# One place more for rounded weight pieces, one fewer for raw weight units, and weight sums taken one unit later

## The chip, the cores and the metric

One core of a Trainium2 chip runs one program. Times are device microseconds of one execution of the whole kernel, the median of several executions. PE is TensorE, DVE is VectorE, ACT is ScalarE, POOL is GpSimd, and SP is the engine that issues most transfers.

## What is computed

Two transformer-like layers over 256 tokens of width 2048, in float32. Everything is a chain of products with weights that are used once, with small attention and recurrence parts between them:

```
proj = rms_norm(x) @ w_in                 # 13 parts: q k v o i f z, two latents, k_r, z_b, g_a, g_b
y_a  = (sigmoid(o) * norm(mlstm(q, k, v)) * silu(z)) @ w_a
y_b  = (attention(latents @ w_uq, latents @ w_ukv) * silu(z_b)) @ w_b
x    = x + (sigmoid(g_a) * y_a + sigmoid(g_b) * y_b) @ w_out
h    = x + concat(fourier_mix, dilated_attention)(rms_norm(x) @ w_in_2) @ w_out_2
h    = h + square(relu(rms_norm(h) @ w_up_2)) @ w_down_2      # d_ff = 8192
out  = rms_norm(h)
```

## The kernel before

**Weights.** All weights are laid out on the host as one stream of 359 units of 1 MB (128 partitions x 2048 floats). SP loads them in order into `raw`, four places. Each unit is cut into pieces of up to 1024 columns, 802 in all. ACT rounds a piece to a float32r high half (L1227, `w_hi`), and DVE subtracts to get the low half (L1827, `w_lo`). PE then makes three products for each block: high x high, high x low, low x high (L659 to L661, L758 to L760). In the feed-forward part ("up" products, `project_up`) it makes one product of twice the width with the high half (L1118) and one with the low half (L1122).

**The ring.** `RING = 4` places hold rounded pieces. The feed-forward part, from piece 490 on, has two places more, `RING_DEEP = 6`, and the last four pieces have places of their own. ACT may round piece n only when PE has used piece n - 4 (n - 6 in the feed-forward part): the wait on `w_used` at L1225. SP loads unit u into the place of unit u - 4 once DVE has made the low halves of that unit's first two pieces (`w_rest`, L496). PE waits for the low half of each piece (`w_rest`).

**Sum units.** In seven pairs of column chunks of the first input product (`pair_in`) and seven pairs of the down product (`pair`), some of the eight steps of a pair replace eight block products by seven, in the manner of Strassen. They need sums of weight blocks, and such a unit has four pieces: a whole and a half piece of raw blocks, and two pieces of sums in `w_sum`. DVE makes the sums with three instructions, `sum_weights` (L1841, L1844, L1845). The kernel before makes the sums of unit u + 1 just behind the low half of the first piece of unit u (L1829). A pair of the down product has sum units at steps 1, 2, 4 and 5 (`SUM_AT`), a pair of the input product at steps 2 and 5 or 3 and 5.

**Order on the engines.** All engines' programs are unrolled and run in order. ACT and DVE go through `pieces(n, slot)`: for each piece that PE uses, they split the piece that stands 4 (6) places ahead, and then do the slot's other work, if any. So the piece that is split beside a given slot, and with it every `sum_weights`, moves when the ring's depth changes; the slot's own place against PE does not.

**Feed-forward part.** Four slabs. Each has eight up chunks (c = 0 to 7) of four pieces, then the down product in two pairs, q = 2n and 2n + 1 (the last slab has one pair and two plain chunks). At the end of an up chunk DVE reads its PSUM banks (L2602, then L2606 squares), and that releases the banks (`proj_read`). The even pair's step 1, its first sum step, writes into banks that chunk 7 used: PE waits there for `proj_read` of all chunks (L1163). At step 5 DVE adds the mixed products (`add_mixed`), and at step 7 ACT drains four banks (`drain_whole`, L1732), before it splits the two pieces of that step. The first two up chunks of the next slab wait for these drains: chunk 0 for the first two (L1181). POOL issues the drained tiles as adding transfers into `nat`.

**Start.** SP's first issues are three units mixed with six parts of the transposed x, a fourth unit, and then the first half of x in natural layout (`nat`), before the loop over the other units.

Of the kernel before, what the change touches and what calls it, by code (L numbers as in the profile page):

```python
# [5 lines left out]
P = 128  # L6
# [11 lines left out]
EPS = 1e-6  # L18
BIG = 1e30
PIECE = 2 * CW  # L20
RING = 4
NORM_FULL = 8
NORM_LORA = 2
NORM_UP = 4
# [3 lines left out]
UNITS = 1 + 4 * (4 + 4 + 8 + 4 + 2 + 8) + 14 + 4 * (4 + 4 + 4) + 4 * 8 + 4 * 4 + 4 * N_SLABS * 8  # L28
# [22 lines left out]
SUM_UNITS = _sum_units()  # L51
# [15 lines left out]
WHERE, FIRST_PIECE = _pieces()  # L67
PIECES = len(WHERE)
DEEP = FIRST_PIECE[UNITS_MLP]
RING_DEEP = RING + 2  # L70


def place_of(piece):

    if piece < DEEP:
        return piece % RING
    if piece >= PIECES - RING:
        return piece % RING + RING_DEEP
    n = (piece - DEEP) % RING_DEEP
    return RING + n if n < 2 else (DEEP + n - 2) % RING  # L80

# [81 lines left out]
def build(nc, stream, x_in, xt_in, consts_in, early_in, params_in, pos_in, dft_in, alibi_in, fg_in, wf_in, z_store, ga_store, gb_store,  # L163
          out):
    f32, f32r, i32 = mybir.dt.float32, mybir.dt.float32r, mybir.dt.int32
# [4 lines left out]
    with ctx:  # L170
# [4 lines left out]
        def place(name, shape, dt, kb):  # L175
            return nc.alloc_sbuf_tensor_at(name, shape, dt, offset=base + int(kb * K))

        raw = place("raw", [P, RING, 2 * PIECE], f32, 0)
        w_hi = place("w_hi", [P, RING, PIECE], f32r, 32)
        w_lo = place("w_lo", [P, RING, PIECE], f32r, 48)  # L180
        a_both = place("a_both", [P, KT, 2, TOK], f32r, 64)
        a_hi, a_lo = a_both[:, :, 0, :], a_both[:, :, 1, :]
        nat = place("nat", [P, TT, D], f32, 96)
# [52 lines left out]
        alibi = place("alibi", [P, H_2, 2 * TOK], f32, 176.25)  # L236
        m_hi = place("m_hi", [P, KT, TOK], f32r, 112)
        m_lo = place("m_lo", [P, KT, TOK], f32r, 128)
        w_hi_end = place("w_hi_end", [P, RING, PIECE], f32r, 64)
        w_lo_end = place("w_lo_end", [P, RING, PIECE], f32r, 80)  # L240
        w_hi_deep = place("w_hi_deep", [P, 2, PIECE], f32r, 144.25)
        w_lo_deep = place("w_lo_deep", [P, 2, PIECE], f32r, 152.25)
        ms_at = [160.25 + 4 * i for i in range(3)] + [190.25]
# [3 lines left out]
        w_sum = place("w_sum", [P, 2, 2 * PIECE], f32, 174.25)  # L247
        fg = place("fg", [P, D], f32, 174.25)
        hi_places = [w_hi[:, i, :] for i in range(RING)] + [w_hi_deep[:, i, :] for i in range(2)]
        hi_places += [w_hi_end[:, i, :] for i in range(RING)]  # L250
        lo_places = [w_lo[:, i, :] for i in range(RING)] + [w_lo_deep[:, i, :] for i in range(2)]
        lo_places += [w_lo_end[:, i, :] for i in range(RING)]

        e_at = 180.25
        early = place("early", [P, N_EARLY], f32, e_at)
# [6 lines left out]
        at = 192.25  # L262
# [4 lines left out]
        at = -(-at * K // 32) * 32 / K  # L267
# [84 lines left out]
        def sem(name):  # L352
            return ctx.enter_context(nc.semaphore(name))
# [3 lines left out]
        early_rounded = sem("early_rounded")  # L357
        early_rest = sem("early_rest")
        early_x = sem("early_x")
        raw_landed = [sem(f"raw_landed{i}") for i in range(RING)]  # L360
        w_rounded = sem("w_rounded")
        w_rest = sem("w_rest")
        w_used = sem("w_used")
# [7 lines left out]
        x_ready = [sem(f"x_ready{i}") for i in range(TT)]  # L371
# [96 lines left out]
        x_v = x_in.rearrange("(t p) d -> p t d", p=P)  # L468
# [4 lines left out]
        @block.sync  # L473
        def _(sp):
            ident_cols = CONSTS["ident"]

            def x_part(i):

                k0, k1 = XT_PARTS[i]
                sp.dma_start(xt[:, k0:k1, :], xt_in[:, k0:k1, :]).then_inc(xt_ready[i], 16)  # L480

            sp.dma_start(raw[:, 0, 0:CW], stream[0][:, 0:CW]).then_inc(first_quarter, 16)
            x_part(0)
            sp.dma_start(raw[:, 0, CW:PIECE], stream[0][:, CW:PIECE]).then_inc(second_quarter, 16)
            x_part(1)
            sp.dma_start(raw[:, 0, PIECE:], stream[0][:, PIECE:]).then_inc(raw_landed[0], 16)
            x_part(2)
            sp.dma_start(raw[:, 1, :], stream[1]).then_inc(raw_landed[1], 16)
            x_part(3)
            sp.dma_start(raw[:, 2, :], stream[2]).then_inc(raw_landed[2], 16)  # L490
            x_part(4)
            x_part(5)
            sp.dma_start(raw[:, 3, :], stream[3]).then_inc(raw_landed[3], 16)
            sp.dma_start(nat[:, 0, :], x_v[:, 0, :]).then_inc(x_ready[0], 16)
            for u in range(RING, UNITS):
                sp.wait_ge(w_rest, FIRST_PIECE[u - RING] + 2)  # L496
                sp.dma_start(raw[:, u % RING, :], stream[u]).then_inc(raw_landed[u % RING], 16)
                if u == RING:
                    sp.dma_start(nat[:, 1, :], x_v[:, 1, :]).then_inc(x_ready[1], 16)
                    sp.dma_start(early[:, :], early_in).then_inc(early_ready, 16)  # L500
                if u == RING + 4:
                    sp.dma_start(cst[:, ident_cols.stop:], consts_in[:, ident_cols.stop:]).then_inc(cst_ready, 16)

            sp.wait_ge(out_ready, 2)
            sp.dma_start(out_v[:, 0, :], nat[:, 0, :]).then_inc(stored, 16)
            for n, c in ((3, 3), (4, 0)):
                cols = slice(c * CW, (c + 1) * CW)
                sp.wait_ge(out_ready, n)
                sp.dma_start(out_v[:, 1, cols], nat[:, 1, cols]).then_inc(stored, 16)
            sp.wait_ge(stored, 16 * 4)  # L510
# [687 lines left out]
        def _(act):  # L1198
            piece, done, chunk, tr, seq = Tally(), Tally(), Tally(), Tally(), Tally()
# [9 lines left out]
            def split(n=1):  # L1209
                for _ in range(n):  # L1210
                    if piece.reg is None and piece.n >= PIECES:
                        return
                    u, at, width, summed = WHERE[piece.n]
                    if piece.n == 1:
                        act.wait_ge(raw_landed[0], 16)
                    elif piece.n == FIRST_PIECE[u]:
                        act.wait_ge(raw_landed[u % RING], (u // RING + 1 if piece.reg is None else piece.cycle(2 * RING)) * 16)
                    src = raw[:, u % RING, at:at + width]
                    if summed:
                        i = SUM_UNITS.index(u)  # L1220
                        act.wait_ge(w_summed, 2 * i + (1 if at == 0 else 2))
                        src = w_sums(i)[:, at:at + width]
                    deep = piece.reg is None and piece.n >= DEEP
                    if not (deep and piece.n >= PIECES - RING):
                        act.wait_ge(w_used, piece.at(RING + 1 - RING_DEEP if deep else 1))  # L1225
                    s = place_of(piece.n) if piece.reg is None else piece.n % RING
                    A(hi_places[s][:, 0:width], src, ACT.Copy).then_inc(w_rounded, 1)  # L1227
                    piece.add()
# [531 lines left out]
            for n in range(N_SLABS):  # L1760
                for c in range(UP_CHUNKS):
# [15 lines left out]
                    b = proj_all[:, 2 * (chunk.n % 2):2 * (chunk.n % 2) + 2, TOK:2 * TOK]  # L1777
# [29 lines left out]
        def _(dve):  # L1807
            piece, done, chunk, tr, seq, his = (Tally() for _ in range(6))
# [8 lines left out]
            def split(n=1):  # L1817
                for _ in range(n):
                    if piece.reg is None and piece.n >= PIECES:
                        return  # L1820
                    u, at, width, summed = WHERE[piece.n]
                    s = place_of(piece.n) if piece.reg is None else piece.n % RING
                    src = raw[:, u % RING, at:at + width]
                    if summed:
                        src = w_sums(SUM_UNITS.index(u))[:, at:at + width]
                    dve.wait_ge(w_rounded, piece.at(1))
                    V.tensor_tensor(lo_places[s][:, 0:width], src, hi_places[s][:, 0:width].bitcast(f32),  # L1827
                                    SUB).then_inc(w_rest, 1)
                    if u + 1 in SUM_UNITS and piece.n == FIRST_PIECE[u]:  # L1829
                        sum_weights(u + 1)  # L1830
                    piece.add()

            def sum_weights(u):

                i = SUM_UNITS.index(u)
                dve.wait_ge(raw_landed[u % RING], (u // RING + 1) * 16)
                b = raw[:, u % RING, :].rearrange("p (b c) -> p b c", b=4)
                s = w_sums(i).rearrange("p (b c) -> p b c", b=4)
                if i > 1:
                    dve.wait_ge(w_rest, FIRST_PIECE[SUM_UNITS[i - 2]] + 4)  # L1840
                V.tensor_tensor(s[:, 0:2, :], b[:, 0:3:2, :], b[:, 3, :].unsqueeze(1).to_broadcast([P, 2, CW]),  # L1841
                                ADD).then_inc(w_summed, 1)
                dve.wait_ge(w_summed, 2 * i + 1)
                chain(V.tensor_tensor(s[:, 2, :], s[:, 0, :], b[:, 2, :], ADD))  # L1844
                V.tensor_tensor(s[:, 3, :], s[:, 2, :], b[:, 1, :], ADD).then_inc(w_summed, 1)  # L1845
# [734 lines left out]
            for n in range(N_SLABS):  # L2580
                for c in range(UP_CHUNKS):
# [18 lines left out]
                    b = proj_all[:, 2 * (chunk.n % 2):2 * (chunk.n % 2) + 2, 0:TOK]  # L2600
# [168 lines left out]
```

## Time and profile before

| | us |
|---|---|
| median of 3 runs | 2095.89 |
| their range | 2095.5 to 2096.8 |
| the profiled execution's own time | 2096.05 |
| its span in the trace | 2094.2 |
| PE busy | 2080.3 |
| DVE busy | 1452.2 |
| ACT busy | 1120.6 |

Read it with care: the matmuls overlap and their ends are modelled, so the busy time of PE does not show a wait shorter than about 0.16 us, the overlap of two neighbours. A steady stream of 512-column products starts one every 0.23 us. The distance between the starts shows what was lost. The part from 1399 us on is the feed-forward part; the pairs of the input product run from about 152 to 449 us.

### The profile page before, as it was taken

Reading aid. Unit: us, or ns where it says so; the run is one execution under the profiler, and the core shown is the slowest. Engines: PE = TensorE matmul, PEld = TensorE weight load, DVE = VectorE, ACT = ScalarE, POOL = GpSimd, SP = SyncE. Lnnn points to the kernel's source line nnn. Section 1 sums busy time; section 2 is a strip of 40 time slices with the busy share of each in tenths; the row PEclk is TensorE's granted clock in tenths of the full one; section 3 lists DMA queues with packets and bytes.
Section 4 is the critical chain, followed back from the end, with each engine's and each line's share of the span. In section 5 each row is a group of like instructions: output and inputs, shape, how many; then the busy total and the mean of one; then the engine's idle time right before and its main releaser. Section 6 shows DMA issues by size and latency. Waiting matters only on the chain.

```text
span 2094.2 us, 25089 instructions
## 1 busy us (share of the span) xinstructions
PE 2080.3 (99%) x10024; PEld 1747.0 (83%) x10024; DVE 1452.2 (69%) x1893; ACT 1120.6 (54%) x1466; POOL 69.5 (3%) x85
## 2 busy tenths in 40 slices
PE   9999999999999999999999999999999999999998
PEld 7888888888888888888888888888888888888886
DVE  6877888875555786556554455566896896797794
ACT  6555555555444675554454454354564565465463
POOL 0000000000000020000000000000010000000000
PEclk9999999999999999999999999999999999999999
DMA  8555455564465544355755542455576477467564
GB/s 334 184 181 209 171 211 210 190 248 177 174 227 201 188 144 161 141 224 198 299 184 185 191 161 101 161 201 182 180 238 232 163 236 237 180 217 256 184 211 133
DMA packets 62196, 413.88 MB, mean 198 GB/s; under 512 B 7040, under 2 KB 7680, under 8 KB 14720
## 3 DMA queue, kind: packets, MB, share of 16 engines
q1 hardware_dynamic: 53856, 382.71, 50.8%
q0 software_dynamic: 7648, 28.84, 4.9%
q8 instruction: 79, 1.29, 0.3%
q10 hardware_dynamic: 576, 0.73, 0.1%
q14 instruction: 37, 0.30, 0.0%
HBM read 394.69 MB, written 8.39 MB: 192 GB/s over the span
## 4 chain that ended last, share of the span: by engine, by line
PE 96%; DVE 1%; ACT 1%; issue 1%; DMA 0%; SPq 0%; POOLq 0%; POOL 0%; DVEq 0%; ACTq 0%
PE proj L659 15%; PE proj L661 15%; PE proj L660 15%; PE proj L1118 11%; PE proj L1122 6%; PE proj L758 4%; PE proj L760 4%; PE proj L759 4%; PE tbank L758 2%; PE tbank L759 2%; PE tbank L760 2%; PE tbank L614 2%; PE bank_a L758 1%; PE bank_a L760 1%; PE bank_a L759 1%; PE bank_b L760 1%
## 5 line engine op out<-in xcount | busy, mean ns | idle before, releaser
L1827 DVE TENSOR_TENSOR w_lo<-raw,w_hi 128x1024 fp32r<-128x1024 f32 (+1 forms) x627 | 740.3, 1195 | 503.3 <-ACT w_hi L1227 496.4
L1227 ACT ACTIVATE w_hi<-raw 128x1024 fp32r<-128x1024 f32 (+1 forms) x627 | 641.9, 1035 | 705.9 <-PE proj L661 463.0
L659 PE MATMUL proj<-w_hi,a_both 128*128 128x512 f32 x1280 | 512.2, 400 | 1.0 <-DVE a_both L1914 0.9
L661 PE MATMUL proj<-w_hi,a_both 128*128 128x512 f32 x1280 | 499.9, 391 | 0.0
L660 PE MATMUL proj<-w_lo,a_both 128*128 128x512 f32 x1280 | 498.4, 389 | 0.0
L661 PEld LDWEIGHTS proj<-w_hi,a_both 128*128 128x128 f32 x1280 | 240.2, 188 | 51.7
L659 PEld LDWEIGHTS proj<-w_hi,a_both 128*128 128x128 f32 x1280 | 240.6, 188 | 48.6 <-DVE a_both L1914 1.8
L660 PEld LDWEIGHTS proj<-w_lo,a_both 128*128 128x128 f32 x1280 | 240.7, 188 | 47.5
L1118 PE MATMUL proj<-a_both,w_hi 128*128 128x512 f32 x672 | 160.7, 391 | 0.3 <-DVE a_both L1873 0.3
L1118 PEld LDWEIGHTS proj<-a_both,w_hi 128*128 128x128 f32 x672 | 123.5, 188 | 24.5 <-DVE a_both L1873 0.5
L1827 DVE TENSOR_TENSOR w_lo_deep<-raw,w_hi_deep 128x1024 fp32r<-128x1024 f32 x86 | 98.3, 1164 | 47.4 <-ACT w_hi_deep L1227 47.3
L1227 ACT ACTIVATE w_hi_deep<-raw 128x1024 fp32r<-128x1024 f32 x86 | 84.3, 1011 | 77.1 <-PE proj L1122 56.4
L1122 PEld LDWEIGHTS proj<-a_both,w_lo 128*128 128x128 f32 x672 | 86.3, 191 | 3.4
L1122 PE MATMUL proj<-a_both,w_lo 128*128 128x256 f32 x672 | 87.3, 283 | 0.0
L1118 PE MATMUL proj<-a_both,w_hi_deep 128*128 128x512 f32 x352 | 84.1, 390 | 0.0
L1118 PEld LDWEIGHTS proj<-a_both,w_hi_deep 128*128 128x128 f32 x352 | 64.7, 188 | 12.6
L758 PE MATMUL proj<-w_hi,a_both 128*128 128x512 f32 x164 | 64.0, 390 | 0.2
L759 PE MATMUL proj<-w_lo,a_both 128*128 128x512 f32 x164 | 63.8, 389 | 0.0
L760 PE MATMUL proj<-w_hi,a_both 128*128 128x512 f32 x164 | 63.8, 389 | 0.0
L1122 PEld LDWEIGHTS proj<-a_both,w_lo_deep 128*128 128x128 f32 x352 | 45.3, 191 | 1.8
L1227 ACT ACTIVATE w_hi<-w_sum 128x1024 fp32r<-128x1024 f32 x38 | 38.8, 1056 | 14.7 <-PE proj L760 5.1
L1827 DVE TENSOR_TENSOR w_lo<-w_sum,w_hi 128x1024 fp32r<-128x1024 f32 x38 | 44.9, 1219 | 2.2 <-ACT w_hi L1227 2.2
(530 smaller groups left out, 3086.3 us busy)
## 6 DMA issues: line engine op xcount, KB each, us to landing
raw<-stream SPq DMA_DIRECT2D x358, 1024.0 KB, 4.8
nat<-stg POOLq DMA_DIRECT2D x35, 256.0 KB, 8.5
nat<-x SPq DMA_DIRECT2D x2, 1024.0 KB, 16.6
z_store<-z POOLq DMA_DIRECT2D x1, 2048.0 KB, 8.3
ga_store<-z POOLq DMA_DIRECT2D x1, 2048.0 KB, 12.2
gb_store<-z POOLq DMA_DIRECT2D x4, 512.0 KB, 7.0
yb<-z_store POOLq DMA_DIRECT2D x4, 512.0 KB, 8.8
ga<-ga_store POOLq DMA_DIRECT2D x1, 2048.0 KB, 8.1
```

Of the source, the lines that this page charges most:

```text
L614: last = nc.tensor.transpose(tbank[(tr.n - aside.n) % 2][:, b * P:(b + 1) * P], src(b), ident)
L659: nc.tensor.matmul(banks[t][:, :], ah, wh, start=first, stop=False)
L660: nc.tensor.matmul(banks[t][:, :], ah, wl, start=False, stop=False)
L661: last = nc.tensor.matmul(banks[t][:, :], al, wh, start=False, stop=end)
L758: nc.tensor.matmul(bank[:, :], hi, wh, start=first, stop=False)
L759: nc.tensor.matmul(bank[:, :], hi, wl, start=False, stop=False)
L760: return nc.tensor.matmul(bank[:, :], lo, wh, start=False, stop=end)
L1118: nc.tensor.matmul(banks[f], hi_places[place_of(piece.n + i)][:, cols], a_both[:, kt, :, :].rearrange("p s t -> p (s t)"), start=(kt == 0) ...
L1122: last = nc.tensor.matmul(banks[f][:, 0:TOK], lo_places[place_of(piece.n)][:, cols], a_hi[:, kt, :], start=False, stop=(kt == KT - 1))
L1227: A(hi_places[s][:, 0:width], src, ACT.Copy).then_inc(w_rounded, 1)
L1827: V.tensor_tensor(lo_places[s][:, 0:width], src, hi_places[s][:, 0:width].bitcast(f32), SUB).then_inc(w_rest, 1)
```

## The change

`RING` goes from 4 to 5, so that the feed-forward part has 7 places. `raw` goes from 4 places to 3 (`RAW`), and the last four pieces keep their own places (`END`). The memory is the same: 8 KB a partition less for `raw`, 4 KB more for each of `w_hi` and `w_lo`. SP issues unit 3 in its loop, behind the wait for the low halves of unit 0, and `nat`'s first half, its second half and the constants each stand behind the same unit as before. The sums of a sum unit are made behind the low half of its own first piece.

```diff
-RING = 4
+RAW = 3
+RING = 5
+END = 4
@@ place_of
-    if piece >= PIECES - RING:
-        return piece % RING + RING_DEEP
+    if piece >= PIECES - END:
+        return piece - (PIECES - END) + RING_DEEP
@@ build
-        raw = place("raw", [P, RING, 2 * PIECE], f32, 0)
-        w_hi = place("w_hi", [P, RING, PIECE], f32r, 32)
-        w_lo = place("w_lo", [P, RING, PIECE], f32r, 48)
+        raw = place("raw", [P, RAW, 2 * PIECE], f32, 0)
+        w_hi = place("w_hi", [P, RING, PIECE], f32r, 24)
+        w_lo = place("w_lo", [P, RING, PIECE], f32r, 44)
@@ sync
-            sp.dma_start(raw[:, 3, :], stream[3]).then_inc(raw_landed[3], 16)
-            sp.dma_start(nat[:, 0, :], x_v[:, 0, :]).then_inc(x_ready[0], 16)
-            for u in range(RING, UNITS):
-                sp.wait_ge(w_rest, FIRST_PIECE[u - RING] + 2)
-                sp.dma_start(raw[:, u % RING, :], stream[u]).then_inc(raw_landed[u % RING], 16)
-                if u == RING:
+            for u in range(RAW, UNITS):
+                sp.wait_ge(w_rest, FIRST_PIECE[u - RAW] + 2)
+                sp.dma_start(raw[:, u % RAW, :], stream[u]).then_inc(raw_landed[u % RAW], 16)
+                if u == RAW:
+                    sp.dma_start(nat[:, 0, :], x_v[:, 0, :]).then_inc(x_ready[0], 16)
+                if u == RAW + 1:
                     sp.dma_start(nat[:, 1, :], x_v[:, 1, :]).then_inc(x_ready[1], 16)
                     sp.dma_start(early[:, :], early_in).then_inc(early_ready, 16)
-                if u == RING + 4:
+                if u == RAW + 5:
@@ vector, split
-                    if u + 1 in SUM_UNITS and piece.n == FIRST_PIECE[u]:
-                        sum_weights(u + 1)
+                    if u in SUM_UNITS and piece.n == FIRST_PIECE[u]:
+                        sum_weights(u)
```

## Rows read from the trace of the kernel before

**Rows 1.** The page: busy engines (part 1) and the ending chain (part 4).
```profile
PE 2080.3 (99%) x10024; PEld 1747.0 (83%) x10024; DVE 1452.2 (69%) x1893; ACT 1120.6 (54%) x1466; POOL 69.5 (3%) x85
...
PE 96%; DVE 1%; ACT 1%; issue 1%; DMA 0%; SPq 0%; POOLq 0%; POOL 0%; DVEq 0%; ACTq 0%
```

**Rows 2.** Waits of PE and ACT: engine, line, releaser, total us, times, longest.
```profile
PE bank_a L697 <- POOL v_a L518: 2.4, 1, 2.4
PE tbank L614 <- ACT x_q L1565: 1.5, 2, 1.4
...
ACT w_hi L1227 <- DMA raw<-stream: 2.7, 3, 1.3
```

**Rows 3.** Timeline of PE, 217.6 to 218.7: start, length, instruction.
```profile
217.63 0.39 PE L760 MATMUL proj<-w_hi,a_both 128*128 128x512 f32 x1
218.10 0.50 PE L758 MATMUL proj<-w_hi,a_both 128*128 128x512 f32 x1
218.44 0.39 PE L759 MATMUL proj<-w_lo,a_both 128*128 128x512 f32 x1
```

**Rows 4.** Timeline of DVE, 214 to 217.
```profile
214.24 1.22 DVE L1841 TENSOR_TENSOR w_sum_vo<-raw 128x1024 f32<-128x1024 f32 x1
215.49 0.69 DVE L1844 TENSOR_TENSOR w_sum_vo<-w_sum_vo,raw 128x512 f32<-128x512 f32 x1
216.21 0.69 DVE L1845 TENSOR_TENSOR w_sum_vo<-w_sum_vo,raw 128x512 f32<-128x512 f32 x1
216.82 2.96 DVE L1827 TENSOR_TENSOR w_lo<-raw,w_hi 128x1024 fp32r<-128x1024 f32 x3
```

**Rows 5.** Timeline of ACT, 1489.
```profile
1489.06 2.02 ACT L1227 ACTIVATE w_hi_deep<-w_sum 128x1024 fp32r<-128x1024 f32 x2 [1.89 <-PE proj L1122]
```

**Rows 6.** Timeline of DVE, 1487.5 to 1494.3.
```profile
1487.55 1.22 DVE L1841 TENSOR_TENSOR w_sum<-raw 128x1024 f32<-128x1024 f32 x1
1488.80 0.69 DVE L1844 TENSOR_TENSOR w_sum<-w_sum,raw 128x512 f32<-128x512 f32 x1
1489.53 0.69 DVE L1845 TENSOR_TENSOR w_sum<-w_sum,raw 128x512 f32<-128x512 f32 x1
1490.13 0.69 DVE L1827 TENSOR_TENSOR w_lo<-raw,w_hi 128x512 fp32r<-128x512 f32 x1
1490.73 1.22 DVE L1827 TENSOR_TENSOR w_lo_deep<-w_sum,w_hi_deep 128x1024 fp32r<-128x1024 f32 x1
1491.87 0.69 DVE L2505 TENSOR_TENSOR m_lo<-stg,m_hi 128x512 fp32r<-128x512 f32 x1
1492.47 1.22 DVE L1827 TENSOR_TENSOR w_lo_deep<-w_sum,w_hi_deep 128x1024 fp32r<-128x1024 f32 x1
1493.61 0.68 DVE L2602 TENSOR_TENSOR stg<-proj,stg 128x512 f32<-128x512 f32 x1
```

**Rows 7.** Timeline of PE, where step 0 of pair 0 ends and step 1 begins.
```profile
1495.00 0.39 PE L760 MATMUL bank_b<-w_hi,m_lo 128*128 128x512 f32 x1
1495.22 0.39 PE L758 MATMUL proj<-w_hi,m_hi 128*128 128x512 f32 x1
```

**Rows 8.** Stretches: us, then busy us of each engine, granted clock, DMA share, GB/s.
```profile
0.00:25.00 25.00, 21.56 (x85) 17.18 (x86) 14.98 (x24) 16.94 (x27) 1.57 (x9) 1.00 0.92 355
...
1500.00:1525.00 25.00, 25.00 (x112) 20.72 (x111) 24.76 (x27) 16.86 (x18) 0.92 (x1) 1.00 0.63 221
1525.00:1550.00 25.00, 25.00 (x112) 20.72 (x111) 24.25 (x28) 15.78 (x18) 3.44 (x4) 1.00 0.76 226
```

**Rows 9.** SP's line L497, the loads of units: time from issue to landing.
```profile
DMA to landing us min/median/max: 4.6/4.8/14.7
```

**Rows 10.** DMA issues from 1569 to 1584: count, size, median us to landing.
```profile
raw<-stream SPq DMA_DIRECT2D x3, 1024.0 KB, 8.1
```

**Rows 11.** Timelines of SP, ACT and PE around the end of pair 1.
```profile
1561.13 0.33 SPq L497 DMA_DIRECT2D raw<-stream  x1
...
1566.14 1.06 ACT L1227 ACTIVATE w_hi<-raw 128x1024 fp32r<-128x1024 f32 x1 [1.60 <-PE proj L760]
1567.57 0.69 ACT L1732 ACTIVATE stg<-proj,inv_sq 128x512 f32<-128x512 f32 x1 [0.36 <-PE proj L760]
1568.87 0.69 ACT L1732 ACTIVATE stg<-proj,inv_sq 128x512 f32<-128x512 f32 x1 [0.61 <-PE proj L760]
...
1571.38 0.84 PE L1118 MATMUL proj<-a_both,w_hi 128*128 128x512 f32 x3
```

**Rows 12.** Timeline of PE after its one wait among the first products.
```profile
12.13 0.50 PE L659 MATMUL proj<-w_hi,a_both 128*128 128x512 f32 x1 [0.85 <-DVE a_both L1914]
12.47 0.39 PE L660 MATMUL proj<-w_lo,a_both 128*128 128x512 f32 x1
```

More of the change, by code:

```diff
@@ L238, in build @@
         m_lo = place("m_lo", [P, KT, TOK], f32r, 128)
-        w_hi_end = place("w_hi_end", [P, RING, PIECE], f32r, 64)
-        w_lo_end = place("w_lo_end", [P, RING, PIECE], f32r, 80)
+        w_hi_end = place("w_hi_end", [P, END, PIECE], f32r, 64)
+        w_lo_end = place("w_lo_end", [P, END, PIECE], f32r, 80)
         w_hi_deep = place("w_hi_deep", [P, 2, PIECE], f32r, 144.25)
@@ L249, in build @@
         hi_places = [w_hi[:, i, :] for i in range(RING)] + [w_hi_deep[:, i, :] for i in range(2)]
-        hi_places += [w_hi_end[:, i, :] for i in range(RING)]
+        hi_places += [w_hi_end[:, i, :] for i in range(END)]
         lo_places = [w_lo[:, i, :] for i in range(RING)] + [w_lo_deep[:, i, :] for i in range(2)]
-        lo_places += [w_lo_end[:, i, :] for i in range(RING)]
+        lo_places += [w_lo_end[:, i, :] for i in range(END)]
         e_at = 180.25
@@ L359, in build @@
         early_x = sem("early_x")
-        raw_landed = [sem(f"raw_landed{i}") for i in range(RING)]
+        raw_landed = [sem(f"raw_landed{i}") for i in range(RAW)]
         w_rounded = sem("w_rounded")
@@ L1216, in split @@
                     elif piece.n == FIRST_PIECE[u]:
-                        act.wait_ge(raw_landed[u % RING], (u // RING + 1 if piece.reg is None else piece.cycle(2 * RING)) * 16)
-                    src = raw[:, u % RING, at:at + width]
+                        act.wait_ge(raw_landed[u % RAW], (u // RAW + 1) * 16)
+                    src = raw[:, u % RAW, at:at + width]
                     if summed:
@@ L1223, in split @@
                     deep = piece.reg is None and piece.n >= DEEP
-                    if not (deep and piece.n >= PIECES - RING):
+                    if not (deep and piece.n >= PIECES - END):
                         act.wait_ge(w_used, piece.at(RING + 1 - RING_DEEP if deep else 1))
@@ L1822, in split @@
                     s = place_of(piece.n) if piece.reg is None else piece.n % RING
-                    src = raw[:, u % RING, at:at + width]
+                    src = raw[:, u % RAW, at:at + width]
                     if summed:
@@ L1835, in sum_weights @@
                 i = SUM_UNITS.index(u)
-                dve.wait_ge(raw_landed[u % RING], (u // RING + 1) * 16)
-                b = raw[:, u % RING, :].rearrange("p (b c) -> p b c", b=4)
+                dve.wait_ge(raw_landed[u % RAW], (u // RAW + 1) * 16)
+                b = raw[:, u % RAW, :].rearrange("p (b c) -> p b c", b=4)
                 s = w_sums(i).rearrange("p (b c) -> p b c", b=4)
```

## The prediction

> **What bounds the kernel now.** I read the page first. PE is busy in 99% of the span and carries 96% of the ending chain [rows 1], so only time in which PE starts no product can be gained. The list of waits comes next. PE's waits are short and none of the long ones is for a weight piece: 2.4 us for a memset at the start, 1.5 us for a copy in the latent part [rows 2]. ACT waited 2.7 us in all for loads [rows 2]. The supply of weights is ahead almost everywhere, and a deeper ring has little to give. What it can give must be read from the distances of matmul starts, since busy time hides a short wait. In steady work two starts lie 0.23 us apart. At 218.10 in the input pairs they lie 0.47 us apart, and the next 0.34 [rows 3]: 0.24 + 0.11 = 0.35 us lost. Then the reader should ask which engine is next: in the down pairs DVE is busy 24.76 of 25 us [rows 8]. There the order of DVE's work decides, and this is what the change alters.
>
> **Part 1, input pairs: a gain of 1.5 us.** The stall at 218.10 has its cause on DVE. The three sum instructions of the next unit (1.22, 0.69 and 0.69 us, from 214.24 to 216.82) stand before the low half of a piece of the unit before [rows 4], and PE took that piece the moment it was ready. With the change the sums stand one unit later, behind the low half of their own unit's first piece, and each piece is rounded one piece (1.4 to 2.7 us of PE work, six or twelve products at 0.23 us) earlier. Both remove the 0.01 us of lateness with room to spare. The pattern occurs four times, in the pairs whose sum steps are 3 and 5 (217.6, 260.2, 302.7 and 345.2 us), 4 x 0.35 = 1.4 us, and a smaller one of 0.14 us at 419 us goes too. Sum: -1.5 us. What is next there is DVE's own unit, low half, sums, half piece: its two sum pieces need 1.14 us of DVE each, and PE has 1.36 us for each, so nothing new is late. The bounds are 0 and -1.6 us; I take -1.5, since the row shows the cause itself.
>
> **Part 2, the even down pairs: a cost of 4.8 us.** This is the term that counts. At the end of up chunk 7 DVE must read the chunk's banks (L2602) before PE can begin step 1 of the pair. Before, this read starts at 1493.61 and takes 0.68 us [rows 6], and the first product of step 1 starts at 1495.22 without a wait [rows 7]: 0.9 us of room. The last unit to be split beside chunk 7 was the pair's first sum unit, and the sums of the second had been made at 1487.55 to 1490.13 [rows 6]. Now the ring is one piece deeper, so beside chunk 7 DVE splits one piece more at the end, and this is the first piece of the second sum unit, behind which its own sums stand now. All of that comes before L2602. In numbers: ACT starts the last two pieces of the chunk at 1489.06, when PE releases a place [rows 5]. With seven places the same release admits pieces 527 and 528 in place of 526 and 527, and DVE, which has nothing else left by then, starts piece 527's low half at about 1490.13. From the distances of the rows: low half 1.14 (1490.73 to 1491.87), L2505 0.60 (1491.87 to 1492.47), low half of 528 1.14 (1492.47 to 1493.61), the three sums 2.58 (1487.55 to 1490.13) [rows 6]. So L2602 starts at 1490.13 + 1.14 + 0.60 + 1.14 + 2.58 = 1495.59 and ends at 1496.27. The first product of step 1 would start at 1496.3, not 1495.22 [rows 7]: 1.1 us late. A wait costs a little more than its length, since the product after it follows at 0.34 us and not 0.23 [rows 3, 12]: +0.1. That makes 1.2 us for each even pair, and there are four (one in each slab, with the same program): 4.8 us. The bounds: nothing, if DVE is earlier than I think by 1.1 us, and 2.6 us for each pair (10.4 us), if the whole sum came on top. The rows give each step, so I take 1.2.
>
> **Part 3, the deeper ring elsewhere: 0.** The slots keep their place against PE, since ACT's split beside a slot waits for the same use of a piece. One more piece ahead covers DVE where it falls behind (24.76 of 25 us busy, [rows 8]), but PE did not wait there before.
>
> **Part 4, three raw places: 0, if landings stay near 5 us.** A unit is now issued two pieces later, so it is 5.4 us later against its use; the extra rounded piece gives back half of that to PE, but not to ACT, which stands in order behind the load. Loads land after 4.8 us in the median [rows 9], and up to 8.1 us beside the adding transfers [rows 10]. ACT's waits of 2.7 us [rows 2] will grow, which costs nothing unless a drain or an eviction stands behind one (below). At the start the landings are the slow ones, 14.7 us at most [rows 9], because the engines are 92% busy [rows 8]: the queue is full. Unit 3 is issued about 5 us later, but behind the same bytes, so it should land when it did. The bounds are 0 and +1 us. I take 0.
>
> The page "DMA: Bandwidth & Descriptors" of the Trainium skill (Rules for kernel authors) says to issue a transfer early and to wait for it late, so that its fixed cost overlaps. This speaks against giving up a raw place. The rows show how much earliness there is to give, and by them the rule costs nothing until landings pass 8 us, which is the first rival.
>
> **The sum.** -1.5 + 4.8 = +3.3 us. Against the profiled execution, 2096.05 + 3.3 = 2099.3, its span 2094.2 + 3.3 = 2097.5. The median stands 0.16 us below that execution, so the median forecast is 2095.89 + 3.3 = 2099.2 us: slower, by 0.16%. A measurement of this kernel can tell about 0.2% (4.2 us) from no change, so this lies inside it.
>
> **Rivals.** (A) *Late raw units in front of the drains at the end of an odd pair*, slower still. Before it drains pair 1, ACT must round piece 574, of unit 265. The load of it now waits for the low half of the last piece of unit 262, at 1561.1, when before unit 266 was issued [rows 11], and it shares the engines with the adding transfers. ACT needs 1.06 us for the piece and two drains at 0.6 us pitch before PE can start the next slab at 1571.4 [rows 11]. So the landing must come by about 1569.2, 8.1 us after the issue: that is the point from which it decides. Beside adding transfers the median was 8.1 us [rows 10]. A landing after 9.2 us would cost 1.1 + 0.3 = 1.4 us at three odd pairs: 2099.2 + 4.2 = 2103.4 us. Against it: at 1561 only one adding transfer runs, not four. (B) *DVE is early enough at chunk 7.* If L2602 keeps its place, for instance since low halves that moved ahead free more of DVE than I count, only the gain of part 1 is left: 2095.89 - 1.5 = 2094.4 us, not slower. For it: 0.9 us of room is there now, and the lateness is only 1.1 us. Against it: ACT's start at 1489.06 is set by PE [rows 5], and nothing behind it can start earlier. (C) *The clock falls at the new waits.* The trace's one wait of this size, 0.85 us at 12 us [rows 12], left the granted clock at 1.00 in its stretch [rows 8]. If the clock fell from its higher level, 2.4 GHz, to 1.2 GHz after each of four waits, a piece of 2.7 us would take 5.4: +11 us for one piece each, 2110 us. The page "TensorE: Matmul & The Clock Gate" of the Trainium skill (HAM oscillation) says that waits between groups of products can throttle the engine again; the trace shows nothing of it here. (D) *The change does nothing that can be seen*: both terms vanish, 2095.9 us.
>
> **How the numbers follow.** The forecast case gets 0.60 and spans 2097.8 to 2100.6 (1.0 to 1.5 us for each even pair, part 4 at 0 to +0.5). A gets 0.17, B 0.13, D 0.05, C 0.01, others 0.04. The range reaches from B to A, 2094.3 to 2103.5. It leaves out C, the others, and the outer parts of A and B, some 0.13 in all. Faster by over 0.2% means under 2091.7: only "others", 0.02. Slower by over 0.2% means over 2100.1: A, C and a quarter of the forecast case, 0.17 + 0.01 + 0.15 = 0.33. The same: 0.65.
>
> **What the profile of the changed kernel would show.** Part 1 is right if the starts near 218 us are 0.23 us apart. Part 2 is right if the list of waits has PE at L758 or its neighbours waiting for DVE L2602 four times, about 171 us apart from 1496 us on, and if the DVE timeline shows L1841 to L1845 right before L2602. If the wait is missing, B holds. If PE waits at L1118 for ACT L1732 three times, A holds. PEclk below 1 after a wait would be C. More time in ACT's waits for raw loads, with no wait of PE behind it, is part 4 as told. The prediction is wrong in kind if PE waits for low halves (L1827) inside the down pairs, where DVE has least to spare.

## The result, and the profile after

The changed kernel takes 2099.7 us in the median of 22 runs (2098.5 to 2101.6). The kernel before, timed beside it, takes 2095.8 (22 runs, 2095.3 to 2097.0). The ratio is 1.0017, 95% interval 1.0012 to 1.0023: slower by 0.17%. The two medians lie 3.9 us apart. The forecast was 2099.2 us with a range of 2094.3 to 2103.5.

| | before | after |
|---|---|---|
| the profiled execution's own time | 2096.05 | 2099.59 |
| its span in the trace | 2094.2 | 2097.0 |
| PE busy | 2080.3 | 2080.2 |
| DVE busy | 1452.2 | 1452.9 |
| ACT busy | 1120.6 | 1115.1 |

Line numbers of the new kernel are higher by 2: L1829 makes low halves, L1229 rounds, L1843 to L1847 make the sums, L2604 reads the banks of an up chunk, L760 to L762 are the products of a sum step.

The busy times of the profile's page say nothing, as expected. The list of waits, the same view as [rows 2], says almost all:

```profile
PE proj L760 <- issue: 4.1, 4, 1.0
PE bank_a L699 <- POOL v_a L520: 2.4, 1, 2.4
PE tbank L616 <- ACT x_q L1567: 1.4, 1, 1.4
```

The first line is new: four waits of 1.0 us at the line that begins a sum step. "issue" means that the profile names no releaser, so the engine that set the end has to be looked for at the same moment. Here are the timelines of PE and of DVE at the first of the four (start, length, instruction), which answer to [rows 7] and [rows 6]:

```profile
1492.51 0.39 PE L762 MATMUL bank_b<-w_hi,m_lo 128*128 128x512 f32 x1
1493.92 0.47 PE L760 MATMUL proj<-w_hi,m_hi 128*128 128x512 f32 x1 [1.02 <-issue]
1494.23 0.39 PE L761 MATMUL proj<-w_lo,m_hi 128*128 128x512 f32 x1
```

```profile
1487.67 1.23 DVE L1829 TENSOR_TENSOR w_lo<-w_sum,w_hi 128x1024 fp32r<-128x1024 f32 x1 [1.98 <-ACT w_hi L1229]
1488.81 0.68 DVE L2507 TENSOR_TENSOR m_lo<-stg,m_hi 128x512 fp32r<-128x512 f32 x1
1489.41 1.22 DVE L1829 TENSOR_TENSOR w_lo<-raw,w_hi 128x1024 fp32r<-128x1024 f32 x1
1490.55 1.22 DVE L1843 TENSOR_TENSOR w_sum<-raw 128x1024 f32<-128x1024 f32 x1
1491.80 0.69 DVE L1846 TENSOR_TENSOR w_sum<-w_sum,raw 128x512 f32<-128x512 f32 x1
1492.53 0.69 DVE L1847 TENSOR_TENSOR w_sum<-w_sum,raw 128x512 f32<-128x512 f32 x1
1493.14 0.68 DVE L2604 TENSOR_TENSOR stg<-proj,stg 128x512 f32<-128x512 f32 x1
```

The reader should see the order on DVE: low half, m_lo, low half, three sums, and only then the read of the banks. It ends at 1493.14 + 0.68 = 1493.82, and PE starts at 1493.92. The two starts of PE lie 1.41 us apart instead of 0.23, and the next two 0.31 us: 1.18 + 0.08 = 1.26 us lost. The other three are alike, at 1664.5, 1836.5 and 2008.5 us: 5.0 us in all.

The five places in the input pairs where before lost 1.5 us are clean. Where [rows 3] showed distances of 0.47 and 0.34 us, PE's timeline is now even:

```profile
217.39 0.39 PE L760 MATMUL proj<-w_hi,a_both 128*128 128x512 f32 x1
217.62 0.39 PE L761 MATMUL proj<-w_lo,a_both 128*128 128x512 f32 x1
217.84 0.39 PE L762 MATMUL proj<-w_hi,a_both 128*128 128x512 f32 x1
```

ACT waits longer for loads. In [rows 2] it was 2.7 us in three waits; now it is 44.9 in 31:

```profile
ACT w_hi L1229 <- DMA raw<-stream: 39.0, 27, 3.9
...
ACT w_hi_deep L1229 <- DMA raw<-stream: 5.9, 4, 2.3
```

### The profile page after: what moved, and what is told of

Read it like the earlier page. It is cut to its first block, busy times and chain, and to the rows that moved or that the text cites. A ratio compares the mean times of both kernels' runs of the same rounds, so it can differ in the third digit from the quotient of the medians.

```text
span 2097.0 us, 25088 instructions
## 1 busy us (share of the span) xinstructions
PE 2080.2 (99%) x10024; PEld 1747.9 (83%) x10024; DVE 1452.9 (69%) x1893; ACT 1115.1 (53%) x1466; POOL 68.8 (3%) x85
## 4 chain that ended last, share of the span: by engine, by line
PE 98%; issue 1%; ACT 1%; DVE 0%; POOL 0%; POOLq 0%; DVEq 0%; ACTq 0%
PE proj L661 15%; PE proj L663 15%; PE proj L662 15%; PE proj L1120 11%; PE proj L1124 6%; PE proj L760 4%; PE proj L762 4%; PE proj L761 4%; PE tbank L760 3%; PE tbank L762 3%; PE tbank L761 3%; PE tbank L616 2%; PE bank_a L762 1%; PE bank_a L761 1%; PE bank_a L760 1%; PE bank_b L762 1%
## 5 line engine op out<-in xcount | busy, mean ns | idle before, releaser
L1829 DVE TENSOR_TENSOR w_lo<-raw,w_hi 128x1024 fp32r<-128x1024 f32 (+1 forms) x647 | 762.9, 1192 | 520.4 <-ACT w_hi L1229 515.3
L1229 ACT ACTIVATE w_hi<-raw 128x1024 fp32r<-128x1024 f32 (+1 forms) x647 | 660.5, 1033 | 690.9 <-PE proj L663 439.0
L1120 PE MATMUL proj<-a_both,w_hi 128*128 128x512 f32 x736 | 177.3, 391 | 0.4 <-DVE a_both L1875 0.4
L1120 PEld LDWEIGHTS proj<-a_both,w_hi 128*128 128x128 f32 x736 | 135.4, 188 | 26.9 <-DVE a_both L1875 0.6
L1829 DVE TENSOR_TENSOR w_lo_deep<-raw,w_hi_deep 128x1024 fp32r<-128x1024 f32 (+1 forms) x66 | 77.3, 1188 | 33.1 <-ACT w_hi_deep L1229 33.1
L1124 PE MATMUL proj<-a_both,w_lo 128*128 128x256 f32 x736 | 97.1, 283 | 0.0
L1229 ACT ACTIVATE w_hi_deep<-raw 128x1024 fp32r<-128x1024 f32 (+1 forms) x66 | 66.7, 1030 | 53.0 <-PE proj L1124 45.9
L1120 PE MATMUL proj<-a_both,w_hi_deep 128*128 128x512 f32 x288 | 70.3, 391 | 0.0
L760 PE MATMUL proj<-w_hi,a_both 128*128 128x512 f32 x164 | 63.8, 389 | 0.0
L762 PE MATMUL proj<-w_hi,a_both 128*128 128x512 f32 x164 | 63.8, 389 | 0.0
L1120 PEld LDWEIGHTS proj<-a_both,w_hi_deep 128*128 128x128 f32 x288 | 52.9, 188 | 10.2
L1229 ACT ACTIVATE w_hi<-w_sum 128x1024 fp32r<-128x1024 f32 x34 | 35.9, 1060 | 47.6 <-DVE w_sum L1843 26.8
L1829 DVE TENSOR_TENSOR w_lo<-w_sum,w_hi 128x1024 fp32r<-128x1024 f32 x34 | 40.8, 1220 | 10.4 <-ACT w_hi L1229 10.4
L661 PE MATMUL proj<-w_hi,lat_hi 128*128 128x512 f32 x112 | 45.7, 408 | 0.4 <-DVE v_b L2365 0.4
```

The lines of the kernel that those rows point to most:

```text
L661: nc.tensor.matmul(banks[t][:, :], ah, wh, start=first, stop=False)
L760: nc.tensor.matmul(bank[:, :], hi, wh, start=first, stop=False)
L762: return nc.tensor.matmul(bank[:, :], lo, wh, start=False, stop=end)
L1120: nc.tensor.matmul(banks[f], hi_places[place_of(piece.n + i)][:, cols], a_both[:, kt, :, :].rearrange("p s t -> p (s t)"), start=(kt == 0) ...
L1124: last = nc.tensor.matmul(banks[f][:, 0:TOK], lo_places[place_of(piece.n)][:, cols], a_hi[:, kt, :], start=False, stop=(kt == KT - 1))
```

## The experiments

They ran in two groups, each on one chip with its own runs of the kernel before: 2095.97 us in the first, 2095.77 in the second. Below, "the loss" at a place is the distance of the starts of PE less 0.23 us, summed over the place.

**The changed kernel with the banks read first** tests part 2 alone: only what DVE does beside up chunk 7 is put in another order.

```diff
@@ vector, split: the sums of a unit
-                        sum_weights(u)
+                        if hold: held.append(u)
+                        else: sum_weights(u)
@@ up chunk 7
+                    if c == UP_CHUNKS - 1: hold.append(1)
                     pieces(NORM_UP, slot=slot)
+                    hold.clear()
...                  # L2602 and L2606 of before
+                    while held: sum_weights(held.pop(0))
```

> The changed kernel, but beside up chunk 7 DVE reads the chunk's banks (and squares them) before it makes the sums of the pair's second sum unit. My theory: PE's four waits of 1.2 us at the first sum step of the even pairs go, 5.0 us in all, and the gain in the input pairs stays: 2099.7 - 5.0 = 2094.7 us, about 1.2 us below the kernel before. Rival, late raw units from the third place given up: the order of DVE's work at chunk 7 does not matter, and the time stays at 2098 to 2100 us.

Measured: 2094.34 us (2093.47 to 2095.77, 11 runs), ratio 0.9993 (0.9984 to 1.0002), and again on the second chip 2094.50 (2093.48 to 2095.80, 11 runs), the same ratio.

> The same kernel as the one with the banks read first, timed again on this chip beside the kernel before, to tell whether its gain can be measured. Theory (parts 1 and the head's gain stay, part 2 is gone): 1.5 us below before, 2094.4, with the ratio's interval below 1 if both sets of runs are put together. Rival (no gain that holds): ratio 1.000, 2095.9.

DVE's timeline in the first of these runs, at the place where the changed kernel lost 1.26 us:

```profile
1489.36 1.22 DVE L1829 TENSOR_TENSOR w_lo<-raw,w_hi 128x1024 fp32r<-128x1024 f32 x1
1490.49 0.68 DVE L2612 TENSOR_TENSOR stg<-proj,stg 128x512 f32<-128x512 f32 x1
...
1491.82 1.22 DVE L1848 TENSOR_TENSOR w_sum<-raw 128x1024 f32<-128x1024 f32 x1
```

The changed kernel started that read at 1493.14. Here it starts 2.6 us earlier, at 1490.49, and the list of PE's waits has no line for a sum step. Each against the kernel before beside it, the changed kernel is 3.9 us above and this one 1.6 below: 5.5 us between them, against 5.0 lost at the four places. So the order of the sums and the bank read is the cause of the loss. It still has three raw places and waits of ACT for loads of 44.7 us in all, so these cost nothing that can be seen here. Its time lies 1.6 and 1.3 us below before on two chips, as expected (1.2 and 1.5). Each interval alone still takes in 1, and one for both sets together is not on record. Of the 22 runs of the two sets, 18 lie below 2095.28 us, the fastest of the 58 runs of before beside them.

**The changed kernel with the sums one unit early**, as before had them, keeps the rings of the change.

```diff
-                    if u in SUM_UNITS and piece.n == FIRST_PIECE[u]:
-                        sum_weights(u)
+                    if u + 1 in SUM_UNITS and piece.n == FIRST_PIECE[u]:
+                        sum_weights(u + 1)
```

> The changed kernel with the sums of a unit made one unit earlier again, as in the kernel before; three raw places and five (seven) rounded ones stay. My theory: the unit split last beside chunk 7 brings no sums of its own with it, so the four waits go, and the input pairs keep their gain by the deeper ring: 2094.3 to 2095 us. Rival, late raw units: DVE now waits earlier for the next unit's landing, so the time is that of the changed kernel or above it, 2099.7 to 2103 us.

Measured: 2096.66 us (2095.93 to 2099.03, 11 runs), ratio 1.0005 (0.9996 to 1.0013), some 2 us above what was expected. The four waits at chunk 7 are gone, but two new ones stand in the input pairs, at 362.0 and 405.4 us. Waits of PE, then the timeline of DVE at the first:

```profile
PE proj L760 <- DVE joined L2125: 0.9, 1, 0.9
PE bank_a L760 <- DVE joined L2125: 0.9, 1, 0.9
```

```profile
359.27 1.22 DVE L1843 TENSOR_TENSOR w_sum_z<-raw 128x1024 f32<-128x1024 f32 x1
360.52 0.69 DVE L1846 TENSOR_TENSOR w_sum_z<-w_sum_z,raw 128x512 f32<-128x512 f32 x1
361.25 0.69 DVE L1847 TENSOR_TENSOR w_sum_z<-w_sum_z,raw 128x512 f32<-128x512 f32 x1
361.85 0.68 DVE L2124 TENSOR_TENSOR joined<-proj,joined 128x512 f32<-128x512 f32 x1
362.57 0.69 DVE L2125 TENSOR_TENSOR joined<-proj,joined 128x512 f32<-128x512 f32 x1
```

It is the same picture at another place: three sums, then the read that releases banks to the next sum step. Each costs 1.22 us, 2.4 together. With the deeper ring, each of the two places of the sums puts them in front of some bank read. That is an effect of the depth together with the order, and neither alone shows it: before has early sums and no such wait. Two more things are to be seen in this trace. The five stalls of 1.5 us are gone here too, so the deeper ring removes them also with the early sums. And DVE waits 5.6 us for loads in front of sums, as the rival said, but PE loses nothing by it in the down pairs: the distances of its starts there are even but for 0.1 us at 1872 us.

**The kernel before with only the later sums**, four raw places and the old ring:

> The kernel before with the one edit that a unit's sums stand behind its own first low half; four raw and four (six) rounded places. My theory: with six places the second sum unit is not split beside chunk 7, so no wait appears there, and the input pairs lose their four waits of 0.35 us: 2095.8 - 1.5 = 2094.3 us. Rival, the place of the sums alone makes the cost: 4 x 1.2 us more than that, 2099 us.

Measured: 2095.96 us (2094.79 to 2097.01, 11 runs), ratio 0.9999 (0.9990 to 1.0008): 1.7 us above what was expected. The rival is refuted, since the trace has no wait at chunk 7. The five stalls of 1.5 us are gone, as expected, but two others are there, at 375.9 (0.11) and at 418 us. Timeline of PE there:

```profile
417.95 0.39 PE L760 MATMUL bank_b<-w_hi,xs_lo 128*128 128x512 f32 x1
418.63 0.50 PE L758 MATMUL proj<-w_hi,xs_hi 128*128 128x512 f32 x1 [0.29 <-DVE w_lo L1827]
418.96 0.40 PE L759 MATMUL proj<-w_lo,xs_hi 128*128 128x512 f32 x1
```

That is 0.56 us, on the low half of the unit's own sums. So 0.67 us are lost again, and of the gain of 1.5 us some 0.85 are left. The spans agree: median 2093.2 us against 2094.1 of before. The time doesn't show it, since what lies around the span was longer in this kernel's runs (median 2.3 us, before 1.8). The last 0.67 us of part 1 need the deeper ring as well. Part 1 of the prediction named it ("each piece is rounded one piece" earlier) but took either as enough, and it called nothing new late.

**The kernel before with only three raw places**, early sums, the old ring:

```diff
-RING = 4   (raw has RING places)
+RING = 4
+RAW = 3    (in short: raw has RAW places; SP's loop, END and the places in memory as in the change)
```

> The kernel before with three raw places in place of four and nothing else: four (six) rounded places, sums one unit early, 8 KB a partition unused. My theory: landings near 4.8 us are early enough, 2095.8 to 2096.8 us, with longer waits of ACT for raw units. Rival, late raw units are a part of the cost: 1 us or more above the kernel before, and a wider spread of its runs than the kernel before has.

Measured: 2100.35 us (2099.78 to 2103.49, 9 runs), ratio 1.0022 (1.0013 to 1.0032). The expectation fell. PE waits for low halves inside the odd down pairs and in the last chunk, which neither before nor the changed kernel does. PE and DVE, first place:

```profile
1547.25 0.39 PE L762 MATMUL proj<-w_hi_deep,m_lo 128*128 128x512 f32 x1
1548.18 0.50 PE L760 MATMUL proj<-w_hi_deep,m_hi 128*128 128x512 f32 x1 [0.55 <-DVE w_lo_deep L1829]
```

```profile
1541.14 1.22 DVE L1829 TENSOR_TENSOR w_lo_deep<-raw,w_hi_deep 128x1024 fp32r<-128x1024 f32 x1
1544.32 1.22 DVE L1843 TENSOR_TENSOR w_sum<-raw 128x1024 f32<-128x1024 f32 x1 [1.97 <-DMA raw<-stream]
1545.58 0.69 DVE L1846 TENSOR_TENSOR w_sum<-w_sum,raw 128x512 f32<-128x512 f32 x1
1546.30 0.69 DVE L1847 TENSOR_TENSOR w_sum<-w_sum,raw 128x512 f32<-128x512 f32 x1
1546.91 1.22 DVE L1829 TENSOR_TENSOR w_lo_deep<-raw,w_hi_deep 128x1024 fp32r<-128x1024 f32 x1
```

DVE stood still 1.97 us in front of the sums, since these need the next unit a whole unit before its own pieces do, and with three places it hasn't landed. In all there are six such waits, 8.9 us. The low half that PE wants queues behind. From 1399 us to the end the losses that before hasn't are 6.0 us, 3.9 of them in the odd pairs and 2.1 in the last chunk. The profiled run was one of the slower ones (2102.36 us), so the median's 4.4 us are less than that.

**Three raw places with the later sums**, the old ring, tells whether the ring or the sums remove that cost:

> The kernel before with three raw places and with the sums behind their own unit's first low half, the ring still four deep (six in the feed-forward part). It is the run with three raw places alone plus the later sums. Theory (three raw places cost 4.4 us only because the early sums make DVE wait for a unit that is issued two pieces later, 8.9 us in six waits, and low halves queue behind that wait; asked for one unit later, the unit has landed): the waits of PE for low halves in the odd down pairs go and the time is that of the late sums alone, 2095 to 2096.5. Rival (the places themselves cost, and only the fifth piece of the deeper ring covers it): 2099 to 2101, as with three raw places alone. The waits for low halves in the last chunk, 2.3 us at 2074 and 2076 us, may stay in both, since no sum unit stands there: in that case 2098.

Measured: 2097.04 us (2095.21 to 2099.07, 11 runs), ratio 1.0006 (0.9997 to 1.0014). It stands 1.3 us above the before beside it, where the early sums stood 4.4 above theirs: 3.1 us less. That lies between the theory's range (up to 2096.5) and the 2098 it gave for the case that the last chunk still waits. DVE has no wait for a load in front of a sum any more, and PE has no loss from 1399 to 2060 us that before hasn't. What stays are the waits in the last chunk, where no sum unit stands; the profiled run (2098.80 us, one of the slower ones) lost 3.9 us by them, against 2.1 with the early sums:

```profile
PE proj L1147 <- DVE w_lo_end L1829: 1.7, 2, 1.3
...
PE proj L1147 <- DVE w_lo_deep L1829: 1.2, 2, 0.6
```

So the theory holds for the odd pairs: the late unit hurt only where DVE asked for it early. Its other branch holds for the last chunk. There the changed kernel shows no loss at all and the run with the banks read first has one short wait in one of its two profiles (0.2 us in the list, 0.4 by the starts), so the deeper ring covers nearly all of it.

**Added work on DVE in front of the bank read** measures the room of part 2 by itself, in the kernel before.

```diff
                     pieces(NORM_UP, slot=slot)
+                    if c == UP_CHUNKS - 1:
+                        for _ in range(2):   # or 6
+                            chain(V.tensor_tensor(k_even[:, :], par[:, 0:TOK], par[:, 0:TOK], ADD))
```

> The kernel before with two added sums on DVE (128x256 each, results not used for anything) in front of L2602 beside up chunk 7 only, four times in the run. Worked out from rows of before: a DVE sum over 128x512 lasts 0.68 us and one over 128x1024 1.22, so 128x256 should last about 0.41, with its chain some 0.45 us; two are 0.9 us. Theory (0.93 us of room between the end of L2602 and the first product of step 1, as 1495.22 less 1494.29): L2602 starts 0.9 later and the first product of step 1 just makes it, at most 0.1 us late: 0 to +0.5 us in all, 2095.9 to 2096.4. Rival (there is no room, what DVE gets in front of L2602 is paid in full): +3.6 us, 2099.5.

> The same with six such sums, 2.7 us more in front of L2602, close to the 2.58 us of three weight sums. Theory: late by 2.7 - 0.93 = 1.8 us, with the surcharge of 0.1 us 1.9 us at each of four places: +7.6 us, 2103.5. Rival (PE waits for the banks at all four, but wins part of it back, since the pieces behind are ready and the pair is not limited by PE alone): +4 us or less. In the trace PE should show four waits for DVE or issue at the first sum step, the first at about 1495 us.

Two additions: 2097.36 us (2096.61 to 2098.76, 11 runs), ratio 1.0007 (0.9998 to 1.0016). The losses at the four places are 0.23, 0.52, 0.23 and 0.23 us, 1.2 in all, and the median rose 1.6: more than the 0 to 0.5 expected. The rival's +3.6 is refuted. DVE's bank read and PE:

```profile
1492.74 0.88 DVE L2601 TENSOR_TENSOR k_even<-par 128x256 f32<-128x256 f32 x2
1493.71 0.69 DVE L2605 TENSOR_TENSOR stg<-proj,stg 128x512 f32<-128x512 f32 x1
```

```profile
1494.13 0.39 PE L760 MATMUL bank_b<-w_hi,m_lo 128*128 128x512 f32 x1
1494.50 0.47 PE L758 MATMUL proj<-w_hi,m_hi 128*128 128x512 f32 x1
```

The read ends at 1494.40 and PE starts at 1494.50. The same 0.10 us stood between them in the changed kernel (1493.82 and 1493.92) and stands there with six additions (1496.71 and 1496.81). So the room is 0.83 us and not 0.93: from the end of the read to the start of the product there is a handover of 0.10 us, which the prediction left out.

Six additions: 2109.04 us (2108.46 to 2111.69, 5 runs), ratio 1.0067 (1.0053 to 1.0080). That is 13.3 us over before, where 7.6 was expected. The waits in the list are near the 1.8 us expected (1.82, 2.10, 1.82 and 1.82), but at three of the four TensorE's clock fell. Timeline of PE, then stretches of time with the granted clock as the third number from the end:

```profile
1496.81 0.47 PE L758 MATMUL proj<-w_hi,m_hi 128*128 128x512 f32 x1 [1.82 <-issue]
1497.12 0.42 PE L759 MATMUL proj<-w_lo,m_hi 128*128 128x512 f32 x1
...
1498.18 0.63 PE L759 MATMUL tbank<-w_lo,m_hi 128*128 128x512 f32 x1
1498.61 0.63 PE L760 MATMUL tbank<-w_hi,m_lo 128*128 128x512 f32 x1
```

```profile
1495.00:1497.00 2.00, 0.19 (x1) 0.22 (x2) 1.81 (x5) 0.00 (x0) 0.00 (x0) 1.00 0.00 0
1497.00:1499.00 2.00, 2.00 (x6) 1.56 (x6) 1.92 (x3) 1.15 (x2) 0.00 (x0) 0.59 0.00 0
1499.00:1501.00 2.00, 2.00 (x7) 1.52 (x6) 1.51 (x3) 1.44 (x2) 0.00 (x0) 0.56 0.30 53
1501.00:1503.00 2.00, 2.00 (x10) 1.68 (x9) 1.88 (x2) 1.51 (x2) 0.00 (x0) 1.00 0.92 389
```

Products start 0.43 us apart and not 0.23: the lower level of the clock, 1.2 GHz and not 2.4. It lasts to 1500.7 and costs some 1.6 us on top of the wait, 3.6 us for this place. At 1668.9, after 2.10 us, the place costs 3.9; at 2016.3 it costs 3.6; at 1843.6, after a wait of 1.82 us as at the first, the clock stayed at its higher level and the place costs 2.1. The four make 13.3 us, which is the measured difference.

## Why the prediction was right, point by point

**Part 1** was right in its size and its place. The five stalls are gone, 1.5 us. The mechanism was less simple than told: the prediction held that either half of the change removes them with room to spare and that nothing new is late. The later sums alone bring 0.85 us, since two other pieces then come late. The deeper ring alone removes all five but brings two waits at the join reads.

**Part 2** was right in the order of DVE's work, instruction by instruction, and nearly in size: 1.26 us for each even pair where 1.2 was forecast, 5.0 for 4.8. The low half that opens the last round starts 4.84 us before PE's last product of step 0 (1487.67 and 1492.51), where the prediction had 4.87 (1490.13 and 1495.00), and from there to the bank read it is 5.47 us (to 1493.14), where it had 5.46. What it left out is the handover of 0.10 us from the read to the product. The surcharge was 0.08 us, where the prediction took 0.11 from its rows. The run with the banks read first shows the cause, and the runs with added work show that the price follows the delay past 0.83 us of room.

**Part 3** put the deeper ring elsewhere at 0. In the changed kernel that missed a gain of 0.5 us (below), and the "0" hid two more effects. The deeper ring puts the early sums in front of the join reads in the input pairs (2.4 us), which the change escapes only because it moves the sums too; and it covers the last chunk, where three raw places otherwise lose 2 to 4 us. A term of 0 was in truth a cover with a price when it is gone.

**Part 4** was right for the change and wrong as a statement about three raw places. By itself that edit costs 4.4 us; the bound was +1. The step that failed is "costs nothing unless a drain or an eviction stands behind one": it looked at ACT's waits only. DVE waits for loads as well, in the sums, and in the down pairs DVE has no time to spare [rows 8]. In the change the later sums take this wait away, and the run with the early sums shows that the deeper ring would have covered it in the down pairs too. The part also read [rows 10] as "up to 8.1 us", which is the median of three loads; by [rows 9] the longest landing was 14.7 us.

**Two small gains were not foreseen.** PE's first wait at 12 us [rows 12] is gone from the profiled execution of the changed kernel, where it runs 0.47 us ahead from there on; the second quarter of unit 0 was rounded at 6.31 us and not at 7.37. The head differs from run to run: in the profile of the later sums alone PE waits 0.7 us there, so this is not put down to the change. The other gain is 0.5 us at four small products with `x_k`, which came late in before. Timeline of PE, before and then after:

```profile
725.98 0.39 PE L661 MATMUL proj<-w_hi,lat_lo 128*128 128x512 f32 x1
727.05 0.50 PE L659 MATMUL proj<-w_hi,lat_hi 128*128 128x512 f32 x1
```

```profile
723.98 0.39 PE L663 MATMUL proj<-w_hi,lat_lo 128*128 128x512 f32 x1
724.57 0.48 PE L661 MATMUL proj<-w_hi,lat_hi 128*128 128x512 f32 x1
```

From one product to the other it is 1.07 us before and 0.59 after. This gain stands in the traces of all four runs with the deeper ring, and in none of the five others beside before, so it goes with the ring. The instruction of POOL ahead of it (`inv_k`) is listed with 2.72 us in the six traces with the old ring and with 1.66 to 1.67 in the four with the deeper one; why is open. Of the two waits for x_q [rows 2], the one of 0.15 us is gone, which is worth 0.06 us by the starts.

If the start of each product is set against that of the same product in before, the whole adds up: -0.5 in the head, -1.5 in the input pairs, -0.5 at 727 us, and 1.30 us at each even pair, since the products right behind the wait lose another 0.04 us: +5.2. The sum is +2.7 us, and the spans give 2.7 to 2.8.

**The median rose by more than the span.** It rose 3.9 us, and the forecast was 3.3. Over 22 runs of the changed kernel the span has a median of 2097.1 us; the kernel before has 2094.1 on the first chip and 2094.0 on the second: 3.0 us. The remaining 0.9 us lies around the span. It is 1.8 or 1.9 us in 47 of the 58 runs of before, and 2.2 to 3.4 in 10 of 22 of the changed kernel. So the forecast of 3.3 us lies as near as it does partly by luck: the terms that the trace shows add up to 2.7, and the part outside the span, which nobody forecast, made up for two gains that were missed. Why is open. The changed kernel's spans also spread more (2096.7 to 2098.8); no trace of a long one was taken.

**The rivals.** A, a late unit in front of the drains, did not happen in the profiled run, but it was near. Timeline of ACT and PE at the end of pair 1, which answers to [rows 11]:

```profile
1567.72 1.06 ACT L1229 ACTIVATE w_hi_deep<-raw 128x1024 fp32r<-128x1024 f32 x1 [2.25 <-DMA raw<-stream]
1568.69 1.25 ACT L1734 ACTIVATE stg<-proj,inv_sq 128x512 f32<-128x512 f32 x2
...
1570.21 2.00 PE L1120 MATMUL proj<-a_both,w_hi 128*128 128x512 f32 x8
```

The unit was issued at 1560.70 and landed after 7.0 us, at 1567.7, and both drains were done at 1569.94, 0.27 us before PE started the next slab. Before had 1.8 us there. The forecast put the point at 8.1 us after the issue; by these rows it is at about 7.3. The prediction took both times from before's rows, but the unit is issued 0.4 us earlier than there (1560.70 for 1561.1) and PE arrives 1.2 us earlier (1570.21 for 1571.4). At the two other odd pairs there were 0.6 and 1.0 us left. A run with slower landings may well lose time here, which would fit the wider spread; that is argued, not shown. B was refuted: DVE did not come early. C, the clock, did not happen after 1.02 us: the granted clock is 1.00 in all stretches around the four waits. The prediction called the 0.85 us at 12 us the trace's one wait of this size, but [rows 2] lists one of 1.4 us as well. It stands at 781 us, between products, and the granted clock is 1.00 in the stretches around it, in before and in every run here. But the run with six additions makes it real. Waits of 1.8 and 2.1 us did bring the lower clock, in three of four places. The rival had named the right danger. It tied it to waits of 1.0 us, where it did not come, and its price of 11 us for four places was too high: the extra was some 1.6 us for each place where the clock fell. The page "TensorE: Matmul & The Clock Gate" of the Trainium skill (HAM oscillation) says that waits between groups of products can throttle the engine again; the trace with six additions agrees, with granted clocks down to 0.50, and the changed kernel's own trace shows nothing of it. D was refuted.

## What to carry to other kernels

On an engine that runs in order, the depth of a ring decides which piece is split beside which other duty, so a deeper ring is also a reordering: after such a change, list what now stands in front of every read that releases PSUM banks, and put those reads first (here this turned a loss of 3.9 us into a kernel 1.3 to 1.6 us below before). A term that comes out as 0 because other work covers it deserves its own experiment: three raw places cost 4.4 us with the old ring and the early sums, the later sums or the deeper ring each remove the part in the down pairs, and only the deeper ring covers the last chunk. Ask for every reader of a load, not only the first one, when it asks.

## What the runs showed of the hardware

From the end of DVE's bank read at chunk 7 to the start of the product that waited for it there were 0.10 us in all three kernels where it could be read, and 0.05 to 0.06 us at the two join reads of the run with the early sums (363.26 and 363.32, 406.70 and 406.76). A wait costs PE more than the list says: the one of 1.02 us took 1.18 us by the distance of the starts, and another 0.08 us since the product behind it followed at 0.31 us; where PE waited for a low half, that surcharge was 0.11 us. The clock's fall was not expected at these lengths. It stayed at the higher level after waits of 1.02 us (four of four), 1.26 and 1.28 us in the last chunk with three raw places, and 1.35 to 1.42 us at the x_q products in all ten traces. It fell at 1.82 us in two of three and at 2.10 us in the one there was, all in one execution.
